# Gate/up biases of a mixture of experts: from matmuls on TensorE to additions on VectorE

## The chip, the cores and the metric

One NeuronCore of a Trainium2 chip runs the whole program, one residual block of an encoder (mixer and mixture of experts) for 512 tokens. The metric is device microseconds of one execution. Five engines work side by side: TensorE (PE; its weight loads are PEld), VectorE (DVE), ScalarE (ACT), GpSimd (POOL) and SyncE (SP), which only issues DMAs here. Semaphores tie them together.

## The reference

Only the experts matter here. Each of 512 tokens goes to 4 of 32 experts; `D_MODEL` and `D_EXPERT` are 1024, all in float32.

```python
    def expert_block(args):
        xb, e = args
        gu = xb @ w_gate_up[e] + b_gate_up[e]
        gate = jnp.minimum(gu[:, ::2], SWIGLU_LIMIT)
        up = jnp.clip(gu[:, 1::2], -SWIGLU_LIMIT, SWIGLU_LIMIT)
        act = (up + 1.0) * (gate * jax.nn.sigmoid(gate * SWIGLU_ALPHA))
        return act @ w_down[e] + b_down[e]
```

`b_gate_up` has 32 x 2048 elements. The change is to how the `+ b_gate_up[e]` is made.

## The kernel before

The first part of the program (the mixer: delta rule, attention, merge of both) ends near 800 us. Then come the router and the tables of which token goes to which expert, up to about 886 us, then the loop over 32 experts, then the tail with the sums over each token's four experts and the last norm.

**An expert.** Up to 96 tokens (`ROWS`), in three groups of 32 (`QUADS`). The gate/up weights come in eight chunks of 1 MB, the down weights in four. All twelve chunks have one place each in the buffer `ring`; SyncE issues the load of a chunk for expert n when a count (`gu_used`, `dn_used`) says that expert n - 1 has used it (`up_weights`, L486, and `down_weights`, L492). TensorE runs `expert(n)` (L1149): `up(n)` (L1106), 8 slices of 12 matmuls of 32 tokens x 512 columns each (each matmul shows as two records in the trace), then `down(n - 1)` (L1135), 96 matmuls of 32 x 256. The four matmuls of one group go to four column strips of the array, so each strip of 32 partitions of the PSUM tile `gu` holds another 512 of the 2048 gate/up columns, for the 32 tokens of the group.

**VectorE.** `activations(n)` (L2145) waits for all eight slices, reads `gu` twice with clamps (L2149 the even columns to `gb`, L2150 the odd ones to `ub`), multiplies, and takes ScalarE's sigmoid (`gate`, from `gb`). The second read releases `gu` for expert n + 1 (`gu_free`). `token_columns` transposes the next expert's gathered tokens in blocks of 32x32, `activation_columns` the activations, as soon as `down(n - 1)` has used the old ones.

**The biases.** In the merge, `bias_part` (L1941) splits the float32 biases three times into bfloat16 parts, which SyncE stores to `bias_dram`. In the expert loop `bias_rows` holds the parts of five experts (15 rows, in each of three groups of partitions); `bias_block` (L503) loads them, block b + 1 while block b is used, into two buffers by turns. After the first slice of `up`, twelve matmuls (L1130) with a 32x32 matrix `pick` of zeros and ones add the expert's three rows to every token's row. VectorE writes `pick` for the next expert (L2153) after its reads of `gu`. Because the buffer is chosen in Python, the loops on SyncE and TensorE are cut into seven.

**GpSimd** gathers the tokens of expert n + 2 from `h_rows` and scatters the outputs of expert n to `expert_rows`, with indirect DMAs.

**The tail.** While `up(31)` runs, SyncE issues the loads of `expert_rows` for the first two of the four slots (L561, 8 x 512 KB), then the four down chunks of expert 31 as `down(30)` uses the old ones, then the rows of the last two slots. VectorE adds the slots up one after the other (`add_slot`, `add_rows`), ScalarE and VectorE norm the result. What some experts have beyond 96 tokens would be done by further blocks (`extra`); here there are none.

The order of work on each engine is as written in the code.

## Time and profile before

| | |
|---|---|
| median of 3 runs | 1935.56 us (1934.43 to 1935.81) |
| span of the profiled execution | 1933.1 us |
| TensorE busy | 1894.0 us, 98% |
| VectorE busy | 587.9 us, 30% |
| ScalarE, GpSimd busy | 333.0 us, 264.1 us |
| DMA, whole span | 497.65 MB, mean 257 GB/s |
| mean granted TensorE clock | 0.990 |

The page gives no time of its own for the profiled execution beside its span. "Busy" counts the time in which an engine executes; for TensorE the ends of matmuls are modelled. The page's slices cut the span in 40 parts of 48.3 us: one digit is the busy share in tenths. A view of waits says who released whom; a landing time is from the issue of a DMA to its completion.

### The profile page before, as it was taken

The numbers are of one execution on the slowest core, as the hardware profiler recorded it, in microseconds if no ns is written. First come the engines' busy times: TensorE is split into PE (matmuls) and PEld (weight loads), VectorE is DVE, ScalarE is ACT, GpSimd is POOL, SyncE is SP. The second block draws the span as 40 slices with busy tenths as digits, with TensorE's granted clock in tenths as the row PEclk, the third lists the DMA queues.
The fourth block names the chain that finished last, engine by engine and source line by source line (L and its number), as shares of the span: only waits on it lengthen the run. The fifth ranks groups of instructions, "written<-read, shape, count | busy, mean of one in ns | idle before, by whom it ended". The sixth has DMA issues, their size and how long they took to land.

```text
span 1933.1 us, 41164 instructions
## 1 busy us (share of the span) xinstructions
PE 1894.0 (98%) x17590; PEld 870.7 (45%) x17590; DVE 587.9 (30%) x1077; ACT 333.0 (17%) x596; POOL 264.1 (14%) x306
## 2 busy tenths in 40 slices
PE   7999999999999999999999999999999999999996
PEld 4455555554555444454343434434343434343434
DVE  2463563635533110144121221212121212121226
ACT  3223323323233000021011010101011101011002
POOL 0010010000100000014122212121212121221200
PEclk9999999999999999997999999999999999999998
DMA  9211011111101322437999999999999999999995
GB/s 377 86 64 48 29 56 33 45 50 44 45 23 66 136 93 68 161 113 279 391 417 405 419 416 405 417 419 404 416 420 414 408 418 419 414 419 418 419 398 225
DMA packets 82948, 497.65 MB, mean 257 GB/s; under 512 B 15543, under 2 KB 16223, under 8 KB 28933
## 3 DMA queue, kind: packets, MB, share of 16 engines
q1 hardware_dynamic: 73364, 480.35, 62.1%
q0 software_dynamic: 9488, 15.94, 2.2%
q8 instruction: 70, 1.15, 0.2%
q14 instruction: 26, 0.21, 0.0%
HBM read 479.47 MB, written 24.92 MB: 261 GB/s over the span
## 4 chain that ended last, share of the span: by engine, by line
PE 93%; DVE 3%; DMA 1%; DVEq 1%; ACT 1%; issue 0%; SPq 0%; ACTq 0%
PE ps L1124 35%; PE ps L621 21%; PE ps L1144 17%; PE ps L616 10%; PE ps L641 2%; PE ps L840 2%; DVE arena L1577 1%; DVE arena L1580 1%; PE ps L1054 1%; DMA arena<-expert_rows 1%; PE ps L958 1%; PE ps L953 1%; PE ps L1130 1%; PE ps L933 0%; PE ps L725 0%
## 5 line engine op out<-in xcount | busy, mean ns | idle before, releaser
L1124 PE MATMUL ps<-arena 128*32 128x512 f32 x5952 | 652.4, 594 | 2.3 <-DVE pick L2153 2.3
L1124 PEld LDWEIGHTS ps<-arena 128*32 128x32 f32 x5952 | 190.7, 110 | 424.4 <-issue 419.3
L621 PE MATMUL ps<-hT,arena 128*128 128x512 f32 x768 | 350.8, 598 | 1.2 <-DVE arena L1580 0.9
L1144 PE MATMUL ps<-arena,hT 128*32 128x256 f32 x6144 | 340.3, 381 | 3.9 <-DMA arena<-in_w_dn 3.9
L1144 PEld LDWEIGHTS ps<-arena,hT 128*32 128x32 f32 x6144 | 201.0, 111 | 150.8 <-issue 25.7
L2149 DVE TENSOR_SCALAR arena<-ps 128x768 f32<-128x768 f32 x32 | 30.6, 958 | 627.4 <-PE ps L1124 627.4
L621 PEld LDWEIGHTS ps<-hT,arena 128*128 128x128 f32 x768 | 139.0, 191 | 144.3 <-issue 140.1
L2306 POOL DMA_INDIRECT expert_rows<-hT,six x90 | 90.4, 1005 | 695.5 <-ACT hT L1215 677.1
L1215 ACT ACTIVATE hT<-arena 128x768 f32<-128x768 f32 x31 | 48.4, 1560 | 443.4 <-DMA arena<-h_rows,gix 443.4
L621 PE MATMUL ps<-arena 128*128 128x512 f32 x256 | 118.5, 603 | 4.4 <-DVE arena L1577 2.2
L2294 POOL DMA_INDIRECT arena<-h_rows,gix x93 | 95.3, 1025 | 49.7 <-POOL gix L2291 27.2
L1215 ACT ACTIVATE arena<-ps 128x512 f32<-128x512 f32 (+4 forms) x114 | 61.4, 539 | 186.5 <-PE ps L840 99.3
L616 PE MATMUL ps<-arena 128*128 128x128 f32 (+3 forms) x352 | 84.5, 370 | 0.0
L1215 ACT ACTIVATE hT<-ps 128x768 f32<-128x768 f32 (+1 forms) x34 | 27.0, 793 | 291.4 <-PE ps L1144 283.2
L2166 DVE STREAM_TRANSPOSE hT<-arena 128x768 f32<-128x768 f32 x32 | 31.3, 978 | 145.7 <-PE ps L1144 145.6
L1577 DVE TENSOR_TENSOR arena<-arena,ps 128x128 f32<-128x128 f32 (+1 forms) x88 | 38.1, 433 | 107.4 <-PE ps L840 57.8
L621 PEld LDWEIGHTS ps<-arena 128*128 128x128 f32 x256 | 46.0, 190 | 53.3 <-issue 46.5
L1577 DVE TENSOR_TENSOR arena<-arena 128x768 f32<-128x768 f32 (+6 forms) x55 | 66.5, 1210 | 6.7 <-issue 4.6
L616 PEld LDWEIGHTS ps<-arena 128*128 128x128 f32 x352 | 52.8, 190 | 21.6 <-issue 17.3
L1580 DVE SCALAR_TENSOR_TENSOR arena<-arena,ps 128x512 f32<-128x512 f32 x24 | 15.6, 679 | 144.1 <-PE ps L616 143.7
L1519 ACT ACTIVATE arena<-arena 128x768 f32<-128x768 f32 x32 | 27.0, 843 | 187.6 <-DVE arena L2149 187.6
L1580 DVE SCALAR_TENSOR_TENSOR arena<-ps,cw,arena 128x511 f32<-128x511 f32 (+2 forms) x72 | 53.7, 745 | 9.2 <-ACT arena L1216 4.7
(254 smaller groups left out, 1289.7 us busy)
## 6 DMA issues: line engine op xcount, KB each, us to landing
arena<-in_w_gu SPq DMA_DIRECT2D x256, 1024.0 KB, 15.9
arena<-in_w_dn SPq DMA_DIRECT2D x128, 1024.0 KB, 15.4
arena<-in_w_pair SPq DMA_DIRECT2D x16, 1024.0 KB, 4.8
arena<-in_w_merge SPq DMA_DIRECT2D x16, 1024.0 KB, 5.0
expert_rows<-oaT SPq DMA_DIRECT2D x4, 2048.0 KB, 25.3
arena<-expert_rows SPq DMA_DIRECT2D x16, 512.0 KB, 13.7
arena<-in_x SPq DMA_DIRECT2D x8, 512.0 KB, 6.7
arena<-in_w_qb SPq DMA_DIRECT2D x4, 768.0 KB, 4.6
```

What stands on the lines that cost most here:

```text
L616: ins = pe.matmul(dst, lhsT, rhs, start=(k == 0), stop=(k == len(pairs) - 1))
L621: ins = pe.matmul(region(name)[:, cols], lhsT, rhs, start=(k == 0), stop=(k == n - 1))
L641: ins = pe.matmul(region(name)[0:m, :], w[:, k, j * P:j * P + m], hT[:, k, :], start=(k == 0), stop=(k == KD - 1))
L840: ins = pe.matmul(region(name)[p, c * CHUNK:(c + 1) * CHUNK], lhs[p, c, :], rhs[p, c, :], start=True, stop=True)
L1124: ins = pe.matmul(gu[32 * j:32 * (j + 1), g, :], columns[:, g, k, :], ring[k][:, 512 * j:512 * (j + 1)], start=(k == 0), stop=(k == KD - 1))
L1144: ins = pe.matmul(yd[32 * j:32 * (j + 1), g, 0:256], aT[:, g, 2 * c + k, :], ring[8 + c][:, D * k + 256 * j:D * k + 256 * (j + 1)], start= ...
L1215: return ac.activation(dst, src, ACT.Copy)
L1577: return dv.tensor_tensor(o, a, b, op)
L1580: return dv.scalar_tensor_tensor(out=o, in0=a, scalar=s, in1=b, op0=op0, op1=op1)
L2166: dv.transpose(aT.rearrange("p g b m -> p (g b m)"), act.rearrange("p g f -> p (g f)")).then_inc(aT_done, 1)
L2294: po.indirect_dma_start(out=xg[:, 256 * g:256 * (g + 1)], out_offset=None, in_=h2_dram.rearrange("r (j d) -> (r j) d", j=4), in_offset=bas ...
L2306: po.indirect_dma_start(out=y_dram.rearrange("r (j d) -> (r j) d", j=4), out_offset=bass.IndirectOffsetOnAxis(ap=six[:, g:g + 1], axis=0), ...
```

## The change

The bias is added by VectorE as it reads `gu`. The host now lays the biases out as columns: `bias_columns` (128 partitions x 32 experts x 16), loaded once. Partition 32 j + r holds, for each of 16 blocks of 32, the element that belongs to place r of strip j. `spread_bias(e)` copies the 16 columns of expert e and runs them through the 32x32 block transpose with a source that repeats each column 32 times (stride 0), so that every partition of strip j ends with the 512 biases of its strip: 256 for gate, 256 for up. `activations` then has two additions (PSUM plus `bias_rows`, repeated for the three groups), and the clamps behind them work in place in SBUF. Gone are the twelve bias products an expert, `pick`, the bfloat16 split, its stores, and all loads of `bias_block`. The loops on SyncE and TensorE are one piece again. The memset of `xg` on GpSimd waits for the end of the mixer instead of the split.

```diff
         def _(sp):
-            sp.dma_start(bfull, b_gu).then_inc(bias_ld, 16)
-            for n in range(4 * PAIRS + 8, 4 * PAIRS + 12):
+            sp.dma_start(bias_columns, b_gu).then_inc(bias_gu_in, 16)
+            for n in range(4 * PAIRS + 8, 4 * PAIRS + 18):
                 mixer_weights(n)
-            for part in range(3):
-                sp.wait_ge(bias_cast, part + 1)
-                sp.dma_start(bias_dram[:, part, :], bpart).then_inc(kept_st, 16)
-                mixer_weights(4 * PAIRS + 12 + 2 * part)
-                mixer_weights(4 * PAIRS + 13 + 2 * part)
...
-            bias_block(1)
-            for b in range(BIAS_BLOCKS):
-                begin = BIAS_EXPERTS * b
-                if b:
-                    up_weights(begin, begin, range(2))
-                    if b + 1 < BIAS_BLOCKS:
-                        bias_block(b + 1)
-                    up_weights(begin, begin, range(2, 8))
-                    down_weights(begin - 1, begin - 1)
-                with sp.Fori(begin + 1 if b else 2, min(begin + BIAS_EXPERTS, NE)) as e:
-                    up_weights(e, e, range(8))
-                    down_weights(e - 1, e - 1)
+            with sp.Fori(2, NE) as e:
+                up_weights(e, e, range(8))
+                down_weights(e - 1, e - 1)
...
         def _(pe):
                     ins.then_inc(gu_used, 1)
-                    if k == 0:
-                        for g in range(QUADS):
-                            for j in range(4):
-                                pe.matmul(gu[32 * j:32 * (j + 1), g, :], pick[32 * g:32 * (g + 1), :], bias_rows[block % 2][32 * g:32 * (g + 1), 512 * j:512 * (j + 1)],
-                                          start=False, stop=False)
...
         def _(dv):
+            def spread_bias(e):
+                dv.tensor_copy(bias_now, bias_columns[:, bass.ds(16 * e, 16)])
+                dv.drain()
+                dv.transpose(bias_rows, bias_now.unsqueeze(2).broadcast_to([P, 16, 32]))
+                dv.drain()
+
-            def activations(n, pick_next=True):
+            def activations(n):
                 dv.wait_ge(gu_used, 8 * n + 8)
-                g2 = gu.rearrange("p g (f two) -> p two (g f)", two=2)
-                dv.tensor_scalar(gb, g2[:, 0, :], LIMIT, None, ALU.min).then_inc(g_min, 1)
-                dv.tensor_scalar(ub, g2[:, 1, :], LIMIT, -LIMIT, ALU.min, ALU.max).then_inc(gu_free, 1)
-                if pick_next:
-                    at = PICK + n + 1 if not isinstance(n, int) or n < NE - 1 else PICK
-                    dv.tensor_copy(pick[:, :], sm[:, bass.ds(at, 1)].broadcast_to([P, 32])).then_inc(pick_done, 1)
+                g2 = gu.rearrange("p g (f two) -> p two g f", two=2)
+                for half, dst in enumerate((gb, ub)):
+                    ins = tt(dst.rearrange("p (g f) -> p g f", g=QUADS), g2[:, half],
+                             bias_rows[:, HALF_F * half:HALF_F * (half + 1)].unsqueeze(1).broadcast_to([P, QUADS, HALF_F]), ALU.add)
+                ins.then_inc(gu_free, 1)
+                dv.drain()
+                dv.tensor_scalar(gb, gb, LIMIT, None, ALU.min).then_inc(g_min, 1)
+                dv.tensor_scalar(ub, ub, LIMIT, -LIMIT, ALU.min, ALU.max)
                 dv.drain()
...
             with dv.Fori(1, NE - 1) as n:
                 activations(n)
                 token_columns(n + 1)
                 activation_columns(n)
+                spread_bias(n + 1)
...
         def _(po):
-            po.wait_ge(bias_cast, 3)
+            po.wait_ge(oa_done, 2 * PAIRS)
             po.memset(xg, 0.0).then_inc(xg_clear, 1)
-            po.memset(bcur, 0.0).then_inc(bias_clear, 1)
```

How the instructions stand on VectorE in the loop over experts 1 to 30. Names are of tiles: `ps` is PSUM (here `gu`), `arena` the SBUF buffer that holds nearly all others, `hT` the transposed or gathered operands. Before:

```order
L2149 TENSOR_SCALAR arena<-ps 128x768
L2150 TENSOR_SCALAR arena<-ps 128x768
L2153 ISA
L2153 COPY pick<-sm 128x32
L1580 SCALAR_TENSOR_TENSOR arena<-arena 128x768
L2157 REGISTER_ALU
L1577 TENSOR_TENSOR arena<-arena 128x3x32x8
L2143 STREAM_TRANSPOSE arena<-hT 128x768
L2165 REGISTER_ALU
L2166 STREAM_TRANSPOSE hT<-arena 128x768
```

and in the changed kernel:

```order
L1525 TENSOR_TENSOR arena<-ps,arena 128x768 x2
L2093 TENSOR_SCALAR arena<-arena 128x768
L2094 TENSOR_SCALAR arena<-arena 128x768
L1528 SCALAR_TENSOR_TENSOR arena<-arena 128x768
L2098 REGISTER_ALU
L1525 TENSOR_TENSOR arena<-arena 128x3x32x8
L2074 STREAM_TRANSPOSE arena<-hT 128x768
L2106 REGISTER_ALU
L2107 STREAM_TRANSPOSE hT<-arena 128x768
L2079 ISA
L2079 COPY arena<-arena 128x16
L2081 STREAM_TRANSPOSE arena<-arena 128x512
```

Two clamps from PSUM have become two additions from PSUM and two clamps in SBUF; the cast to `pick` is gone from the middle, and copy and transpose of the next expert's bias stand at the end, behind the transpose that waits for `down(n - 1)`.

On SyncE's queue, at the step from one block of five experts to the next, before:

```order
L544 COMPARE_AND_BRANCH
L490 DMA arena<-in_w_gu 128x2048 x2
L511 DMA csn<-bias_parts 16x2048 x3
L490 DMA arena<-in_w_gu 128x2048 x6
L496 DMA arena<-in_w_dn 128x2048 x4
```

The three bias loads stood between the second and the third chunk of the block's first expert. In the changed kernel the whole of it is one loop of eight `in_w_gu` and four `in_w_dn` loads an expert, and its last lines are followed by the tail:

```order
L508 REGISTER_ALU
L508 COMPARE_AND_BRANCH
L511 DMA hT<-in_norm_final 128x1024
L518 DMA arena<-in_token_row 128x512
L525 DMA arena<-expert_rows 128x1024 x8
L486 DMA arena<-in_w_dn 128x2048 x4
L525 DMA arena<-expert_rows 128x1024 x8
```

No load of the tail has moved against another.

## Rows read from the trace of the kernel before

**Rows 1.** the page's slices of the span, 40 equal ones: TensorE, DMA engines, rate

```profile
PE   7999999999999999999999999999999999999996
DMA  9211011111101322437999999999999999999995
GB/s 377 86 64 48 29 56 33 45 50 44 45 23 66 136 93 68 161 113 279 391 417 405 419 416 405 417 419 404 416 420 414 408 418 419 414 419 418 419 398 225
```

**Rows 2.** timeline of TensorE, one expert: start us, us, engine, line, operation

```profile
1074.89 18.23 PE L1124 MATMUL ps<-arena 128*32 128x512 f32 x168
1092.94 10.54 PE L1144 MATMUL ps<-arena,hT 128*32 128x256 f32 x192
1103.30 2.76 PE L1124 MATMUL ps<-arena 128*32 128x512 f32 x24
1105.99 0.42 PE L1130 MATMUL ps<-csn,pick 32*32 32x512 bf16 x12
1106.34 18.23 PE L1124 MATMUL ps<-arena 128*32 128x512 f32 x168
```

**Rows 3.** waits of TensorE, whole run: us in total, times, longest

```profile
PE ps L1144 <- DMA arena<-in_w_dn: 3.9, 1, 3.9
```

**Rows 4.** DMA issues in 945:977, 1400:1450, 1816:1850; last number: us to landing

```profile
arena<-in_w_gu SPq DMA_DIRECT2D x8, 1024.0 KB, 8.1
...
arena<-in_w_gu SPq DMA_DIRECT2D x12, 1024.0 KB, 16.0
...
arena<-in_w_gu SPq DMA_DIRECT2D x9, 1024.0 KB, 20.6
```

**Rows 5.** timeline of the tail, DMA queue and VectorE

```profile
1882.00 8.10 SPq L496 DMA_DIRECT2D arena<-in_w_dn  x4
...
1889.77 0.98 DVE L2166 STREAM_TRANSPOSE hT<-arena 128x768 f32<-128x768 f32 x1 [5.81 <-PE ps L1144]
...
1906.08 4.87 DVE L1580 SCALAR_TENSOR_TENSOR oaT<-arena,w,oaT 128x1024 f32<-128x1024 f32 x4 [2.63 <-DMA arena<-expert_rows]
```

**Rows 6.** timeline of the DMA queue, one block's bias load

```profile
1172.46 1.36 SPq L511 DMA_DIRECT2D csn<-bias_parts  x3
```

**Rows 7.** stretches of the loop: us, TensorE busy, its clock, DMA share, GB/s

```profile
1019.00:1025.00 6.00, 6.00 (x64) 1.00 1.04 324
1176.00:1184.00 8.00, 8.00 (x80) 1.00 1.02 337
1184.00:1198.00 14.00, 14.00 (x232) 1.00 1.01 420
1334.00:1344.00 10.00, 10.00 (x96) 1.00 1.02 338
1491.00:1505.00 14.00, 14.00 (x164) 1.00 1.02 367
1650.00:1661.00 11.00, 11.00 (x128) 1.00 1.01 402
```

**Rows 8.** the same view, stretches of the tail

```profile
1863.00:1878.00 15.00, 15.00 (x148) 1.00 0.99 389
1878.00:1894.00 16.00, 12.11 (x213) 0.96 0.96 360
```

**Rows 9.** groups by line and shape, VectorE, one expert, then the tail

```profile
L2149 DVE TENSOR_SCALAR arena<-ps 128x768 f32<-128x768 f32 x1 | 1.0, 958 | 20.1 <-PE ps L1124 20.1
...
L2143 DVE STREAM_TRANSPOSE arena<-hT 128x768 f32<-128x768 f32 x1 | 1.0, 979 | 0.1
...
L1577 DVE TENSOR_TENSOR oaT<-oaT,ps 128x768 f32<-128x768 f32 x4 | 3.8, 955 | 1.0 <-issue 1.0
```

**Rows 10.** timeline of TensorE, first slice of expert 1

```profile
912.89 4.48 PE L1124 MATMUL ps<-arena 128*32 128x512 f32 x24 [2.30 <-DVE pick L2153]
```

**Rows 11.** stretches around it, TensorE and its clock

```profile
913.00:917.00 4.00, 4.00 (x24) 0.57 0.93 286
917.00:921.00 4.00, 4.00 (x48) 1.00 0.62 214
```

More of the change, by code:

```diff
@@ L181, in build @@
         weight_dram = nc.dram_tensor("choice_weights", [SEQ * NE, 1], F32, kind="Internal").ap()
-        bias_dram = nc.dram_tensor("bias_parts", [NE, 3, 2 * DE], BF16, kind="Internal").ap()
         mk = sb("mk", [P, N_MASKS, P])
@@ L362, in build @@
         gate_done, merged = sem("gate_done"), sem("merged")
-        wo_in, row_in, bias_ld, bias_cast, kept_st = (sem(n) for n in ("wo_in", "row_in", "bias_ld", "bias_cast", "kept_st"))
+        wo_in, row_in, bias_gu_in, kept_st = (sem(n) for n in ("wo_in", "row_in", "bias_gu_in", "kept_st"))
         x2_done, h2_done, h2_st, x2T_done = (sem(n) for n in ("x2_done", "h2_done", "h2_st", "x2T_done"))
@@ L496, in down_weights @@
                     sp.dma_start(ring[c], w_dn_chunk(e, c)).then_inc(chunk_in[c], 16)
-            def up_bias(n, e):
-                sp.wait_ge(gu_used, 8 * n + (2 - 8))
-                for g in range(QUADS):
-                    sp.dma_start(bcur[32 * g:32 * g + 3, :], bias_dram[bass.ds(e, 1)].rearrange("o b f -> (o b) f")).then_inc(bias_gu_in, 16)
-            def bias_block(b):
-                rows = 32 if b == 1 else min(3 * BIAS_EXPERTS + 1, 3 * (NE - BIAS_EXPERTS * b))
-                if b == 1:
-                    sp.wait_ge(list_done, 1)
-                    sp.wait_ge(gu_used, 8)
-                if b > 1:
-                    sp.wait_ge(gu_used, 8 * (BIAS_EXPERTS * (b - 1) - 1) + 2)
-                for g in range(QUADS):
-                    sp.dma_start(bias_rows[b % 2][32 * g:32 * g + rows, :], bias_dram.rearrange("e b f -> (e b) f")[3 * BIAS_EXPERTS * b:3 * BIAS_EXPERTS * b + rows, :]).then_inc(bias_gu_in, 16)
             up_weights(0, 0, range(6))
-            sp.wait_ge(kept_st, 48)
-            sp.wait_ge(bias_clear, 1)
-            bias_block(0)
             def keep_rows(t):
@@ L1104, in weight_columns, with up @@
                 fill(ins, "wm")
-            def up(n, beside={}, picked=True, block=0):
+            def up(n, beside={}):
                 if not first(n):
@@ L1111, in up @@
                     pe.wait_ge(xT_done, n)
-                if first(n):
-                    pe.wait_ge(bias_gu_in, 16 * QUADS)
-                if picked:
-                    pe.wait_ge(pick_done, n + 1)
-                else:
-                    pe.wait_ge(bias_gu_in, 16 * QUADS * n - 16 * QUADS * (NE - BIAS_BLOCKS - 1))
                 for k in range(KD):
@@ L1126, in up @@
                     ins.then_inc(gu_used, 1)
-                    if k == 0:
-                        for g in range(QUADS):
-                            for j in range(4):
-                                pe.matmul(gu[32 * j:32 * (j + 1), g, :], pick[32 * g:32 * (g + 1), :], bias_rows[block % 2][32 * g:32 * (g + 1), 512 * j:512 * (j + 1)],
-                                          start=False, stop=False)
                     if k in beside:
@@ L1147, in down, with expert @@
                     ins.then_inc(dn_used, 1)
-            def expert(n, block=0):
-                up(n, block=block)
+            def expert(n):
+                up(n)
                 down(n - 1)
@@ L1159, in _ @@
             expert(1)
-            for b in range(BIAS_BLOCKS):
-                if b:
-                    pe.wait_ge(bias_gu_in, 16 * QUADS * (b + 1))
-                with pe.Fori(BIAS_EXPERTS * b if b else 2, min(BIAS_EXPERTS * (b + 1), NE)) as n:
-                    expert(n, b)
+            with pe.Fori(2, NE) as n:
+                expert(n)
             down(NE - 1)
@@ L2168, in _ @@
             token_columns(1)
-            dv.wait_ge(kept_st, 64)
+            dv.wait_ge(kept_st, 16)
+            dv.wait_ge(bias_gu_in, 16)
+            spread_bias(0)
             activations(0)
             activation_columns(0)
+            spread_bias(1)
             with dv.Fori(1, NE - 1) as n:
@@ L2213, in _ @@
                     with dv.If(j < extra):
+                        e = dv.value_load(lst[0:1, bass.ds(j + LIST, 1)], min_val=0, max_val=NE - 1)
+                        spread_bias(e)
                         token_columns(j + NE)
-                        activations(j + NE, pick_next=False)
+                        activations(j + NE)
                         activation_columns(j + NE)
@@ L2359, in constants @@
     small = np.zeros((P, SMALL + 4 * EXTRA), np.float32)
-    row = np.arange(P)[:, None] % 32
-    holds = np.where(row < 3 * BIAS_EXPERTS, row // 3, -1)
-    small[:, PICK:PICK + NE] = (holds == np.arange(NE)[None, :] % BIAS_EXPERTS) & (np.arange(P)[:, None] < 32 * QUADS)
     small[:, 128:128 + ROWS] = np.arange(ROWS).reshape(QUADS, 32)[:, ::-1].reshape(-1)
@@ L2405 @@
                       for j in range(KD)])
+    bias = np.asarray(b_gate_up)[0].reshape(NE, 4, 8, 32, 2).transpose(1, 3, 0, 4, 2).reshape(P, NE * 16)
     data = dict(
```

38 lines of the change are left out of this document (9 added, 29 removed).

## The prediction

> **What bounds the kernel now.** I read the page first: of 40 slices of the span, TensorE is at 9 tenths in nearly all, and from slice 20 on the DMA engines are too, at 400 to 420 GB/s [rows 1]. So the second half, the 32 experts, has two resources near full, and the question is which one the change relieves, and which one sets the end.
>
> The timeline of TensorE in one expert answers for TensorE [rows 2]. From 1074.89 to 1106.34, one expert takes 31.45 us, with no gap in the rows. Its parts: seven of eight slices of the gate/up products take 1092.94 - 1074.89 = 18.05 us (2.58 each), the down products 10.36, and the first slice with the twelve bias products behind it 1106.34 - 1103.30 = 3.04. The seven others cost 2.58, so the bias products cost 0.46 us on TensorE. In the whole loop TensorE waits for DMA once, in the last down products, 3.9 us [rows 3]. Up to there TensorE sets the pace.
>
> The DMA view answers for the loads. A weight load of 1 MB lands 8.1 us after its issue at 945 to 977 us, 16.0 at 1400 to 1450, and 20.6 at 1816 to 1850 [rows 4]. A load waits only for the ring slot to come free, so the landing time is the backlog of the DMA engines. It grows over the loop and nowhere drops back: from about 945 us the DMA engines always have work, and TensorE takes weights a little faster than they come. What TensorE lives on is the ring of twelve chunks: a chunk is asked for when the expert before has used it and is needed one period less one slice later, 31.45 - 2.58 = 28.9 us. Of that 8.3 us are left at the end. So the last down weights and the slot rows behind them, asked for from 1882 us on, stand in a queue that has not been empty for 900 us, and the final sums on VectorE start when slot rows land, at 1906.08 after a wait of 2.63 [rows 5]. The end of the kernel is therefore set by the **sum of the DMA work**, although TensorE is "98% busy".
>
> **What the change does, part by part.**
>
> *Bias products off TensorE.* 32 experts x 0.46 = 14.7 us of TensorE's path [rows 2]. They stood in the chain in every expert, so TensorE reaches its last down products 14.7 us sooner if nothing else stops it. The new period is 30.99 us.
>
> *Bias loads off the queue.* Six blocks of experts follow the first; five of their loads fall into the saturated time, three issues each, 16 rows x 4 KB an issue, that is 0.197 MB a block (the fifth 6 rows, 0.074 MB) [rows 6]. They cost far more than their bytes. Beside 420 GB/s in a quiet stretch, the stretches in which they land move 324, 337, 338, 367 and 402 GB/s over 6, 8, 10, 14 and 11 us [rows 7]. Lost bytes: 0.58, 0.66, 0.82, 0.74, 0.20 MB; with the bias's own bytes 0.77, 0.86, 1.02, 0.94, 0.27, and at 420 GB/s 1.8, 2.1, 2.4, 2.2, 0.7 us, together 9.2. The first and the last of these stretches also hold rows of gathers and scatters, which pass at a slightly lower rate, so I take 8.6. Bounds: by bytes alone 0.86 MB, 2.1 us; at most 9.2.
> The Trainium skill (SBUF — State Buffer, the DMA port swizzle) says that a load's rate depends on how many of 16 ports its partitions reach, four for partitions 0 to 15, about 109 GB/s, and that partitions 32 further on share them. By it the two loads on the same ports would take 0.131 MB / 109 GB/s = 1.2 us a block, 5.3 us in all, and the time would come out at 1927.7; the trace agrees in kind (a fifth of the rate gone for some ten us) and asks more.
>
> *Where these two meet.* Since the backlog never empties, a load less is worth its time at the end, and TensorE's 0.46 an expert is worth nothing there beyond the point where the backlog begins. What TensorE gains before it counts: two experts' bias products (0.92) and the step between the first two experts (below, 0.1 to 0.2), 1.1 us together. Then the tail: the last down weights are issued at 1882.00 because TensorE's progress releases them [rows 5], and in 1878 to 1894 the engines move only 360 GB/s, beside 389 just before [rows 8]; some of them had run dry. With TensorE 14.7 us ahead and the backlog deeper this hole closes: (389 - 360) x 16 / 389 = 1.2 us, and against the 420 GB/s of a quiet stretch 2.3; I take 1.5, nearer to the row beside it.
>
> *Does TensorE run dry?* Backlog growth from 8.1 to 20.6 is 12.5 us in some 28 experts, 8.6 of it the bias loads, leaving 0.14 an expert. At a period of 30.99 it becomes 0.14 + 0.46 = 0.60 an expert, 17 us in 28, so about 25 us at the end of the 28.4 that the ring allows. It is close, and only a stall earlier than the last two experts would cost anything new.
>
> *VectorE's new work.* Per expert: the two reads of PSUM become additions with a second operand. A tensor_tensor of 128x768 with one operand in PSUM takes 955 ns in the tail, beside 958 for the clamp that reads PSUM now [rows 9]; no change. The two clamps move to SBUF: between half and all of 958 ns each. A copy of 16 columns stands in for a cast of 32 columns, nothing; the transpose of 128x512 is below the 979 ns of one of 128x768 [rows 9]. Sum: at most 2 x 0.96 + 0.98 = 2.9 us more, on an engine that waits 20.1 us of the period for the products. The cover: products of expert n are read while the down products of n - 1 run, 10.36 us, and gate/up banks are freed after the two additions, 1.9 us, as now. The spreading stands behind the transpose of the activations and before a wait of 20 us. In the last expert VectorE waits 5.81 us with its product done [rows 5]; the clamps' 1.9 fit. Only between experts 0 and 1 nothing covers: TensorE waited 2.30 us for the two reads and the cast there [rows 10]; without the cast 0.1 to 0.2 less.
>
> *Before the experts.* The three splits of the biases on VectorE and their stores stand beside the merge's matmuls, and of TensorE's waits only one is for a DMA [rows 3]. Nothing is gained, and the single load of columns is as large as the one it replaces.
>
> **Sum:** 8.6 + 1.1 + 1.5 = 11.2 us. The profiled execution has a span of 1933.1, 2.5 below the median of 1935.56; the page gives no other time for it, so I take these 2.5 as lying around the span. Predicted: span 1921.9, time 1924.4.
>
> **Rivals.**
> 1. *TensorE's path sets the end after all* (the tail follows the last down products, not the slot rows). For it: TensorE's gap-free timeline. Against it: VectorE waited for rows, not for TensorE. Gain 14.7 + 0.2, time 1920.7.
> 2. *Bias loads cost little more than their bytes* (the dips are something else that stays, such as the fetch of code at a loop's end). 2.1 + 1.1 + 1.5 = 4.7, time 1930.9. Against it: the dips come at each of the five blocks, and the smallest block has the smallest.
> 3. *Nothing to measure*: the deeper backlog makes the slot rows of the tail land late by as much as the loads gave back, and the bias terms are at their lower bound: 2.1 + 1.1 and no hole closed, less what the rows lose; time 1932 to 1936. Against it: the queue serves in order, and its sum is smaller.
> 4. *Slower*: the ring's 28.4 us are used up long before the end; TensorE waits in each expert, and behind a wait its clock is low. Behind the wait of 2.30 us the first slice took 4.48 us [rows 10], beside 2.58: the granted clock is 0.57 in 913 to 917 us, so mostly the 1.2 GHz level, and 1.00 from 917 on [rows 11]. That is 1.9 us an expert lost on TensorE's own path, which ends at 1920.7 without it; eight such experts make it a loss, twelve give 1920.7 + 12 x 1.9 = 1943.5. Against it: the ring would have to be used up by expert 20, from 8.1 to 28.4 us, 1.0 an expert instead of 0.60, and each slow slice lets the loads catch up.
>
> **Chances.** DMA work sets the end, as forecast: 0.60 (own range 1921.5 to 1928). Rival 1: 0.18. Rival 2: 0.14. Rival 3: 0.04. Rival 4: 0.04. What can be told from no change is about 0.2%, 3.9 us. Range for 8 in 10: from rival 1's 1920.7, less the 0.7 us by which two of the runs may differ, 1920.0, to 1930.0, which leaves out the last us of rival 2, and rivals 3 and 4. Faster by over 0.2%: 0.60 + 0.18 + 0.13 of rival 2 = 0.91; same: 0.01 + 0.04 = 0.05; slower 0.04.
>
> **What would show it.** Right: a period of 31.0 us between slices of successive experts; landing times that climb evenly, without steps, to 22 to 27 us; no dips below 390 GB/s in the loop; TensorE waiting more than 3.9 us for the last down weights; VectorE's last slot sum starting about 11 us sooner. Wrong: a TensorE wait inside the loop before expert 29 (rival 4), a climb below 20 us (rival 1), dips that remain (rival 2), or a period above 31.2, which would say that the bias products had been cheaper than 0.46.

## The result and the profile after

| | before | after |
|---|---|---|
| median | 1935.68 us (1934.43 to 1935.81) | 1923.64 us (1921.35 to 1925.91) |
| ratio | | 0.9936, 95% interval 0.9924 to 0.9948 |
| span of the profiled execution | 1933.1 us | 1923.9 us (that execution took 1925.91) |
| TensorE busy | 1894.0 us | 1877.7 us |
| VectorE busy | 587.9 us | 634.5 us |
| DMA | 497.65 MB | 495.45 MB |

12.0 us less, 0.6%. Forecast were 1924.4 us and a range of 1920 to 1930.

The page's slices of the span after (TensorE, DMA engines, rate), beside [rows 1]:

```profile
PE   7999999999999999999999999999999999999995
DMA  9211111111101412337999999999999999999995
GB/s 374 89 66 31 43 45 50 45 51 44 45 10 39 177 66 88 116 131 275 370 420 418 420 417 419 418 420 419 417 420 418 420 418 420 418 419 419 418 400 210
```

By the busy digits nothing has changed: both are at 9, as before. The third row has. In the loop it read 404, 405, 408 where the bias loads passed; now it stays at 417 to 420.

TensorE's timeline of one expert, beside [rows 2]:

```profile
1070.48 20.81 PE L1081 MATMUL ps<-arena 128*32 128x512 f32 x192
1091.08 10.57 PE L1096 MATMUL ps<-arena,hT 128*32 128x256 f32 x192
1101.44 8.79 PE L1081 MATMUL ps<-arena 128*32 128x512 f32 x80
```

One expert now takes 1101.44 - 1070.48 = 30.96 us instead of 31.45. The down products take 10.36 as before, the eight slices 20.60 instead of 21.09.

TensorE's waits, beside [rows 3] and [rows 10]:

```profile
PE ps L1096 <- DMA arena<-in_w_dn: 8.9, 1, 8.9
...
PE ps L1081 <- DVE arena L1525: 2.3, 1, 2.3
```

In the expert loop there is still one wait for weights, for the last down products, and it has grown from 3.9 to 8.9 us: TensorE reached its end earlier, the weights not as much. (A new one of 0.6 us stands ahead of the experts, for `in_w_cq`.) Between experts 0 and 1 TensorE waits for the additions as it had waited for the cast.

DMA issues in 945:977, 1400:1450 and 1780:1830, the last number being the time to landing, beside [rows 4]:

```profile
arena<-in_w_gu SPq DMA_DIRECT2D x8, 1024.0 KB, 9.1
...
arena<-in_w_gu SPq DMA_DIRECT2D x11, 1024.0 KB, 16.5
...
arena<-in_w_gu SPq DMA_DIRECT2D x14, 1024.0 KB, 24.3
```

The backlog of the DMA engines ends higher than before (20.6), though less is loaded: TensorE uses weights faster.

The tail, SyncE's queue, VectorE and TensorE, beside [rows 5]:

```profile
1867.93 8.10 SPq L486 DMA_DIRECT2D arena<-in_w_dn  x4
...
1876.13 8.20 SPq L525 DMA_DIRECT2D arena<-expert_rows  x8
...
1884.53 12.07 PE L1096 MATMUL ps<-arena,hT 128*32 128x256 f32 x192 [8.88 <-DMA arena<-in_w_dn]
...
1896.85 4.87 DVE L1528 SCALAR_TENSOR_TENSOR oaT<-arena,w,oaT 128x1024 f32<-128x1024 f32 x4 [7.46 <-DMA arena<-expert_rows]
```

The last down weights are asked for 14.1 us sooner (1882.00 before), but the sum of the third slot starts only 9.2 us sooner (1906.08 before), behind a wait of 7.46 us instead of 2.63. Everything behind it is as long as before. So 14 us gained on TensorE have become 9 here (12 by the medians), and the rest is waiting for DMA.

Rates at the place of one former bias load, then in three stretches before VectorE's wait for slot rows ends at 1896.85: the 50 us that end 10 us before it, those 10 us, and the whole last 50 (us, TensorE busy, its loads, VectorE, ScalarE, GpSimd, clock, DMA share, GB/s), beside [rows 7, 8], first after:

```profile
1176.00:1184.00 8.00, 8.00 (x81) 2.86 (x74) 0.00 (x0) 1.57 (x1) 0.00 (x0) 1.00 1.02 419
...
1837.00:1887.00 50.00, 41.12 (x552) 21.65 (x548) 21.94 (x27) 3.21 (x4) 3.02 (x3) 0.94 0.99 399
1887.00:1897.00 10.00, 10.00 (x180) 6.13 (x176) 2.54 (x3) 0.34 (x1) 0.00 (x0) 0.97 0.74 297
1847.00:1897.00 50.00, 41.12 (x564) 21.43 (x560) 18.93 (x22) 2.00 (x3) 2.53 (x3) 0.93 0.93 374
```

then before, at the same distances from that addition:

```profile
1846.00:1896.00 50.00, 46.11 (x632) 20.48 (x628) 16.85 (x22) 3.31 (x4) 3.01 (x3) 0.97 0.99 391
1896.00:1906.00 10.00, 10.00 (x156) 5.81 (x152) 7.34 (x7) 0.00 (x0) 0.00 (x0) 0.82 1.01 400
1856.00:1906.00 50.00, 46.11 (x616) 20.75 (x612) 18.80 (x21) 2.46 (x3) 3.01 (x3) 0.93 0.99 388
```

The dip of 337 GB/s is gone. The tail's hole has not closed, it has moved. Up to 10 us before the addition (399 - 391) x 50 / 417 = 1.0 us are gained, and in the last 10 us (400 - 297) x 10 / 417 = 2.5 us are lost: the DMA engines were busy for 0.74 of that time, before for all of it. Over the whole 50 us after stands (388 - 374) x 50 / 417 = 1.7 us worse. So the last part of the 7.46 us of waiting is not behind a full queue. The share is a mean over 16 engines; that some were idle already while others still moved parts of the third slot's rows would fit it, but the trace does not name the engines.

VectorE's forms after (line, shapes, count | busy, mean ns | idle before), beside [rows 9]:

```profile
L1525 DVE TENSOR_TENSOR arena<-ps,arena 128x768 f32<-128x768 f32 x64 | 58.3, 953 | 584.2 <-PE ps L1081 584.2
...
L2081 DVE STREAM_TRANSPOSE arena<-arena 128x512 f32<-128x512 f32 x32 | 22.8, 711 | 2.4
...
L2093 DVE TENSOR_SCALAR arena<-arena 128x768 f32<-128x768 f32 x32 | 17.9, 560 | 3.0
L2094 DVE TENSOR_SCALAR arena<-arena 128x768 f32<-128x768 f32 x32 | 17.8, 555 | 0.0
```

An addition from PSUM costs 953 ns, what the clamp from PSUM had cost (958); a clamp in SBUF 0.56 us. VectorE's new work is 2 x 0.56 + 0.71 + 0.13 = 1.96 us an expert.

### The profile page after: what moved, and what is told of

Same layout as the page of the kernel before. It is cut to its first block, busy times and chain, and to the rows that moved or that the text cites. A ratio compares the mean times of both kernels' runs of the same rounds, so it can differ in the third digit from the quotient of the medians.

```text
span 1923.9 us, 40758 instructions
## 1 busy us (share of the span) xinstructions
PE 1877.7 (98%) x17206; PEld 948.9 (49%) x17206; DVE 634.5 (33%) x1168; ACT 333.3 (17%) x596; POOL 262.0 (14%) x305
## 2 busy tenths in 40 slices
DMA packets 82217, 495.45 MB, mean 258 GB/s; under 512 B 15188, under 2 KB 15868, under 8 KB 28256
## 4 chain that ended last, share of the span: by engine, by line
PE 92%; DVE 3%; DMA 1%; DVEq 1%; SPq 1%; ACT 1%; issue 1%; ACTq 0%
PE ps L1081 34%; PE ps L584 21%; PE ps L1096 17%; PE ps L579 10%; PE ps L604 2%; PE ps L803 2%; DMA arena<-expert_rows 1%; DVE arena L1525 1%; DVE arena L1528 1%; PE ps L1017 1%; PE ps L921 1%; PE ps L916 1%; PE ps L896 0%; PE ps L688 0%; PE ps L773 0%
## 5 line engine op out<-in xcount | busy, mean ns | idle before, releaser
L1081 PEld LDWEIGHTS ps<-arena 128*32 128x32 f32 x5952 | 233.4, 110 | 396.5 <-issue 393.0
L1096 PEld LDWEIGHTS ps<-arena,hT 128*32 128x32 f32 x6144 | 240.2, 110 | 115.2 <-issue 27.6
L1525 DVE TENSOR_TENSOR arena<-ps,arena 128x768 f32<-128x768 f32 x64 | 58.3, 953 | 584.2 <-PE ps L1081 584.2
L1525 DVE TENSOR_TENSOR arena<-arena 128x768 f32<-128x768 f32 (+5 forms) x53 | 62.0, 1172 | 6.2 <-issue 0.2
```

Source lines behind the costliest of these rows:

```text
L1081: ins = pe.matmul(gu[32 * j:32 * (j + 1), g, :], columns[:, g, k, :], ring[k][:, 512 * j:512 * (j + 1)], start=(k == 0), stop=(k == KD - 1))
L1096: ins = pe.matmul(yd[32 * j:32 * (j + 1), g, 0:256], aT[:, g, 2 * c + k, :], ring[8 + c][:, D * k + 256 * j:D * k + 256 * (j + 1)], start= ...
L1525: return dv.tensor_tensor(o, a, b, op)
```

## The experiments

**Theory:** two paths end close together. One is the sum of the DMA work, the other TensorE's products with VectorE's sums behind them. The later one sets the end, so undoing one half of the change should lift one path only. **Rivals:** TensorE's time counts in full (and the loads for their bytes), or the bias loads count for everything. Medians of before, which ran beside each group of experiments, were 1935.36, 1935.64, 1935.92 and 1936.27 us. Every experiment is an edit of the kernel after. "Over after" is against its 1923.64.

| kernel | edit | us | ratio to before, 95% | over after |
|---|---|---|---|---|
| after_again | none | 1923.60 | 0.9937, 0.9923 to 0.9950 | 0.0 |
| e0_both | products and loads back | 1933.98 | 0.9988, 0.9980 to 0.9997 | 10.3 |
| e1_loads | bias loads back | 1934.15 | 0.9989, 0.9980 to 0.9997 | 10.5 |
| e2_products | products back, 32 experts | 1933.45 | 0.9984, 0.9975 to 0.9993 | 9.8 |
| e2_half | products back, experts 2 to 15 | 1923.88 | 0.9944, 0.9932 to 0.9957 | 0.2 |
| e3_vector | spreading four times | 1924.17 | 0.9935, 0.9920 to 0.9950 | 0.5 |
| e1_wide | loads: 1 x 128 partitions x 1.5 KB | 1926.62 | 0.9959, 0.9946 to 0.9973 | 3.0 |
| e1_full3 | loads: 3 x 128 x 512 B | 1926.58 | 0.9957, 0.9943 to 0.9970 | 2.9 |
| e1_three | loads: 3 x 64 x 1 KB | 1933.00 | 0.9987, 0.9978 to 0.9996 | 9.4 |
| e1_strided | loads: 3 x 16 x 4 KB, 8 apart | 1931.19 | 0.9975, 0.9966 to 0.9984 | 7.5 |
| e4_tail | third slot by tiles | 1920.27 | 0.9923, 0.9909 to 0.9937 | -3.4 |
| e4_order | e4_tail, down weights first | 1926.45 | 0.9950, 0.9936 to 0.9963 | 2.8 |

A figure "over after" is good to about 2 us, and to about 3 where only five executions stand behind it (e1_wide, e1_full3, e4_tail, e4_order). By the ratios, which compare each kernel with its own before, e2_half comes to 1.5 over after, e1_wide and e1_full3 to 4.5 and 4.1, and the three other forms of the loads (e1_strided, e1_three, e1_loads) to 7.5, 9.9 and 10.3.

### The loads alone

```diff
+            def spent_block(b):
...
+                for g in range(QUADS):
+                    sp.dma_start(spare[32 * g:32 * g + rows, :], x[3 * 16 * b:3 * 16 * b + rows, :]).then_inc(spent_in, 16)
...
-            with sp.Fori(2, NE) as e:
-                up_weights(e, e, range(8))
-                down_weights(e - 1, e - 1)
+            for b in range(7):
+                begin = 5 * b
+                if b:
+                    up_weights(begin, begin, range(2))
+                    if b + 1 < 7:
+                        spent_block(b + 1)
...
```

> The changed kernel with the bias loads of blocks 1 to 6 put back (same issues, same rows of 4 KB, same places in the queue, to a buffer that nobody reads; the rows are rows of x). TensorE has no bias products. Theory (the sum of the DMA work sets the end): the loads cost at the end what they cost the queue, 8.6 us or a little more, so 1923.6 + 8.6 = 1932.2; the landing time climbs in steps again and reaches the ring's 28.4 us near expert 24, and TensorE waits inside the loop. Rival 1 (TensorE's path sets the end): the loads are hidden, 1923 to 1925. Rival 2 (bias loads cost their bytes only): 2.1 us, 1925.7.

1934.15 us. TensorE's waits for weights, then the landing of gate/up weights in 1400:1450 and 1780:1830, then the sum of the third slot, in e1_loads:

```profile
PE ps L1117 <- DMA arena<-in_w_dn: 11.1, 1, 11.1
...
PE ps L1102 <- DMA arena<-in_w_gu: 1.6, 7, 0.3
```

```profile
arena<-in_w_gu SPq DMA_DIRECT2D x12, 1024.0 KB, 21.8
...
arena<-in_w_gu SPq DMA_DIRECT2D x12, 1024.0 KB, 27.9
```

```profile
1903.00 4.87 DVE L1549 SCALAR_TENSOR_TENSOR oaT<-arena,w,oaT 128x1024 f32<-128x1024 f32 x4 [9.68 <-DMA arena<-expert_rows]
```

Landing climbs until the ring is used up (27.9 of 28.4 us); then TensorE waits, 1.6 us in seven small pieces. The loads alone bring the end back to within 1.2 us of before, with TensorE still fast. TensorE's gain is worth almost nothing while they are there.

### The products alone, in all experts and in fourteen

```diff
                     ins.then_inc(gu_used, 1)
+                    if k == 0 and products:
+                        for g in range(QUADS):
+                            for j in range(4):
+                                pe.matmul(gu[32 * j:32 * (j + 1), g, :], pick[32 * g:32 * (g + 1), :], spent[32 * g:32 * (g + 1), :], start=False, stop=False)
...
```

Both operands are zeros.

> The changed kernel with twelve bf16 products of zeros behind the first slice of every expert, as before the change; no bias loads. Theory: TensorE reaches the last down products 15 us later, its 8.9 us of waiting there are used up and the rest shows, with the 1.1 us of the first experts: 1923.6 + 15.5 - 8.9 + 1 = about 1931; the landing time at the end of the loop is about 12 us instead of 24.9. Rival 1 (TensorE's path sets the end in full): 1923.6 + 15.5 = 1939. Rival (products are free because the queue is the bound alone): 1924.

> The same twelve products of zeros, but in experts 2 to 15 alone: 14 x 0.49 = 6.9 us on TensorE. Theory: 6.9 is less than the 8.9 us that TensorE waits for the last down weights, so the end stays within 1 us, 1923.6 to 1924.6, and that wait falls from 8.9 to about 2 us. Rival 1 (TensorE's path): 1930.5.

With the products in every expert, 1933.45 us, where about 1931 was expected. The theory had counted the 8.9 us that TensorE waits in after as slack, but the distance between the two ends was 15.7 - 9.8 = 5.9 us. That is nearer to VectorE's wait of 7.46, less the 1.4 us that VectorE waits longer here for TensorE's late products in the tail (1.68 instead of 0.25). Landing in 1400:1450 and 1780:1830, and the tail:

```profile
arena<-in_w_gu SPq DMA_DIRECT2D x12, 1024.0 KB, 8.6
...
arena<-in_w_gu SPq DMA_DIRECT2D x11, 1024.0 KB, 9.8
```

```profile
1891.51 10.57 PE L1101 MATMUL ps<-arena,hT 128*32 128x256 f32 x192 [1.15 <-ACT hT L1168]
1894.24 4.87 DVE L1533 SCALAR_TENSOR_TENSOR oaT<-arena,w 128x1024 f32<-128x1024 f32 x4
1899.24 9.87 DVE L1533 SCALAR_TENSOR_TENSOR oaT<-arena,w,oaT 128x1024 f32<-128x1024 f32 x8
```

The backlog hardly grows (8.9 us at 945:977, 9.8 at the end, where about 12 was expected), no engine waits for DMA in the tail, and the three early sums stand back to back. Here the other path is seen undisturbed: down products of expert 30, the transpose behind them, sums. It ends at 1933.45, and without 32 x 0.49 = 15.7 us of products it would, as an estimate, end at 1917.8. The growth of 12.5 us in the landing before [rows 4] came nearly all from the bias loads: with the same period and no loads it is 0.9.

With the products in experts 2 to 15 only, 14 x 0.49 = 6.9 us of TensorE time cost 0.2 us by the medians (1.5 by the ratios), far from the 6.9 of rival 1. TensorE's wait for the last down weights fell from 8.9 to 1.3 us, close to the 2 expected. Landing in the same two windows, and the third slot:

```profile
arena<-in_w_gu SPq DMA_DIRECT2D x11, 1024.0 KB, 9.3
...
arena<-in_w_gu SPq DMA_DIRECT2D x12, 1024.0 KB, 16.7
```

```profile
1894.66 4.87 DVE L1535 SCALAR_TENSOR_TENSOR oaT<-arena,w,oaT 128x1024 f32<-128x1024 f32 x4 [0.24 <-DMA arena<-expert_rows]
```

The wait for slot rows has shrunk from 7.46 to 0.24 us: both paths end together here. The third slot's rows landed no later than in after, although TensorE had released their loads later.

### Both back

The edit is those of e1_loads and e2_products together.

> Both put back: the bias loads of blocks 1 to 6 and the twelve products of zeros in every expert. Theory: the kernel before in all that costs time, so its time within 1 us, 1935 to 1936.5; the two alone give 8.6 and 7.5 of 12, so they must not add up (8.6 + 7.5 = 16). Rival (something else of the change made part of the gain: the uncut loops, the split in the merge): below 1933.

1933.98 us, landing 18.7 us in 1780:1830. Alone the two cost 10.5 and 9.8, together 10.3. That is the later of two ends, not a sum. The theory had wanted 1935 to 1936.5, the rival below 1933, and the result lies between them. What is still missing to before (1935.36 beside it) is 1.4 us by the medians and 2.3 by the ratio, whose interval, 0.9980 to 0.9997, leaves out 1. So a small part of the gain comes from something that no run put back (the bias split in the merge and its stores are candidates); which, stays open.

### VectorE's work

```diff
-                dv.transpose(bias_rows, bias_now.unsqueeze(2).broadcast_to([P, 16, 32]))
-                dv.drain()
+                for _ in range(4):
+                    dv.transpose(bias_rows, bias_now.unsqueeze(2).broadcast_to([P, 16, 32]))
+                    dv.drain()
```

> The kernel after with the block transpose that spreads the bias made four times instead of once in every expert, 3 x 0.71 = 2.1 us more VectorE work in each of 32 experts (67 us in the whole), at the place where the prediction said that it is hidden (before a wait of 18.78 us for the products). Theory, nothing changes: 1923 to 1924.5, the wait shrinks to 16.7 us, the period stays 30.96. Rival, VectorE's additional work of the change does lie on the path somewhere in each expert: 30 x 2.1 = 63 us slower for all of it, or some 6 us for a tenth of it. Between experts 0 and 1, where nothing covers VectorE, the spreading stands ahead of expert 0's products and should not show either.

1924.17 us. VectorE's timeline of one expert in e3_vector:

```profile
1215.79 1.82 DVE L1525 TENSOR_TENSOR arena<-ps,arena 128x768 f32<-128x768 f32 x2 [16.41 <-PE ps L1081]
...
1227.26 3.07 DVE L2082 STREAM_TRANSPOSE arena<-arena 128x512 f32<-128x512 f32 x4
```

67 us more work changed nothing that can be told; the wait for the products took it (18.78 us in after, 16.41 here).

### Why a load of 0.2 MB costs 2 us

The forecast had priced these loads by the dips, without a reason for them. Five runs (e1_loads and four more) with the same bytes at the same places of the queue ask for it. The first block, near 911 us, has twice the rows in each form: in e1_loads its loads go to 32 partitions, in e1_strided to 32 that lie 4 apart.

```diff
e1_wide
+                sp.dma_start(spare[:, 0:24 * rows], x.rearrange("a (b c) -> (a b) c", c=1024)[P * (b % 4):P * (b % 4) + P, 0:24 * rows]).then_inc(spent_in, 16)
e1_strided
+                    sp.dma_start(spare[at:at + step * (rows - 1) + 1:step, :], x[3 * 16 * b:3 * 16 * b + rows, :]).then_inc(spent_in, 16)
e1_three
+                    sp.dma_start(spare[64 * (g % 2):64 * (g % 2) + 64, 512 * (g // 2):512 * (g // 2) + 16 * rows], x[64 * ((b + g) % 8):64 * ((b + g) % 8) + 64, 0:16 * rows]).then_inc(spent_in, 16)
e1_full3
+                    sp.dma_start(spare[:, 256 * g:256 * g + 8 * rows], x[P * ((b + g) % 4):P * ((b + g) % 4) + P, 0:8 * rows]).then_inc(spent_in, 16)
```

> The kernel after (1923.64) with the same bytes that the bias loads moved (0.197 MB for a block, 0.393 for the first), at the same places of SyncE's queue and in a loop cut into the same seven pieces, but as one load over all 128 partitions instead of three over 16 partitions each. e1_loads, with three loads over 16 partitions each, took 1934.15, 10.5 more than after. Theory: what cost time was that few partitions were written. Then only the bytes are left, 0.86 MB at 420 GB/s, 2.1 us, and a fetch of rows that is none worse than a weight's: 1925.7 to 1926.5, no stretch of the loop far below 400 GB/s. Rival A, it is the cut loops and waits on SyncE's queue or the number of loads: as e1_loads, 1933 to 1935 for the cuts, and between the two if it goes by the number of loads (three against one): 1927 to 1929. The output is the reference's; the loaded rows are used by nothing.

> As e1_loads (three loads a block, 16 rows of 4 KB each), but each load's 16 rows go to 16 partitions 8 apart (start 0, 4 and 1) instead of 16 in a row, so bytes, number of loads, rows and row size are the same and only the places in SBUF differ. Theory A, neighbouring partitions are what is slow (the Trainium skill, SBUF — State Buffer, the DMA port swizzle, says that partitions 0 to 15 reach only four of 16 ports): the cost falls well below the 10.5 us of e1_loads, to about half or less, 1926 to 1929. Theory B, what is slow is 16 rows of 4 KB in one load, however they are placed, because such a load occupies the DMA engines unevenly: the cost stays, 1933 to 1935. The output is the reference's; the loaded rows are used by nothing.

> As e1_loads (three loads at each of the six places, 0.197 MB together, the same cut loops), but each load goes to 64 partitions with 1 KB each instead of 16 partitions with 4 KB each. So far: one load over 128 partitions costs 3.0 us against after (e1_wide, 1926.62), three over 16 partitions 8 apart cost 7.5 (e1_strided, 1931.19), three over 16 neighbouring partitions 10.5 (e1_loads, 1934.15). Theory, a load is dear when it writes few partitions with long rows: three loads over 64 partitions cost little more than the one over 128, 1926.5 to 1928. Rival, the number of loads makes the larger part of the 7.5 that e1_strided still costs: 1929.5 to 1931.5. The output is the reference's; the loaded rows are used by nothing.

> Three loads at each of the six places, as in e1_loads and e1_three, with the same bytes together, but each goes to all 128 partitions with 512 bytes each. e1_three (three loads over 64 partitions) took 1933.00, so its theory of few partitions with long rows fell, and e1_wide (one load over 128) took 1926.62. They differ in the number of loads and in whether a load covers all 128 partitions. Theory A, a load over a part of the partitions is what slows the weights beside it (a weight load covers all 128, and in the trace of e1_three the stretch in which its loads pass moves 290 to 383 GB/s with the engines busy all the time): three loads over all partitions cost little more than one, 1926 to 1928, and no stretch falls below 390 GB/s. Theory B, the number of loads does it: 1931 to 1934, with dips as in e1_three. The output is the reference's; the loaded rows are used by nothing.

One load over all 128 partitions cost 3.0 us, so the cut loops were not it. Spreading the 16 rows helped by 3 of 10.5 us, less than half: neither theory of e1_strided held. Then 64 partitions cost 9.4, not to be told from 10.5, and the theory of few partitions with long rows fell with it. Three loads over all partitions cost 2.9, no more than one. What remains is one distinction: **a load over all 128 partitions cost about its bytes, the same bytes over some of them 2.5 to 3.5 times as much by the medians** (1.7 to 2.5 times by the ratios). The two wide kernels' intervals reach down to 0.9946 and 0.9943, that of after up to 0.9948, so their 3 us are not sharp; after_again, at 1923.60, says that after itself had not moved. At 417 GB/s all the bytes take 3.0 us with the block loaded near 911 us (0.39 + 0.86 = 1.25 MB) and 2.1 us without it, as the forecast had them; the runs cannot tell these apart. The stretch in which the loads of one block pass, 1175:1187 us (us, TensorE busy, its loads, VectorE, ScalarE, GpSimd, clock, DMA share, GB/s), in e1_loads, e1_strided, e1_three, e1_full3 and e1_wide:

```profile
1175.00:1187.00 12.00, 12.00 (x148) 5.67 (x144) 3.23 (x5) 2.43 (x2) 0.00 (x0) 1.00 1.02 354
```

```profile
1175.00:1187.00 12.00, 12.00 (x160) 6.12 (x156) 4.14 (x6) 2.41 (x2) 0.00 (x0) 1.00 1.01 377
```

```profile
1175.00:1187.00 12.00, 12.00 (x128) 4.89 (x124) 1.00 (x2) 1.58 (x1) 0.74 (x2) 1.00 1.02 362
```

```profile
1175.00:1187.00 12.00, 12.00 (x176) 6.76 (x172) 5.78 (x7) 2.42 (x2) 0.00 (x0) 1.00 1.02 419
```

```profile
1175.00:1187.00 12.00, 12.00 (x181) 6.91 (x177) 6.35 (x7) 2.29 (x2) 0.00 (x0) 1.00 1.01 421
```

The DMA share is the same in all five: the engines are busy all the time, only each byte takes longer. That holds for the weights beside the bias too: by the trace's records of single packets, a weight packet of 8 KB in this stretch took 371 ns on average in e1_loads, 349 in e1_strided and 366 in e1_three, beside 315 in e1_full3, 314 in e1_wide and 317 in after.
The Trainium skill (SBUF — State Buffer, the DMA port swizzle and the section on issuing two DMAs) says that partitions 0 to 63 reach only 8 of 16 ports and that only one transfer spanning all 128 reaches all 16. The order of e1_three and e1_full3 agrees in kind. Its figures do not cover the size of e1_three: at half the rate the bytes would take twice their 3.0 us, so it would cost an estimated 6.0 us, and it cost 9.4. For e1_loads, with 4 ports for 16 partitions and 8 for the first block's 32, the same reckoning gives an estimated 3.0 x (2 x 0.39 + 4 x 0.86) / 1.25 = 10.1 us, and it cost 10.5. By the ports of e1_full3, all 16, nothing is lost, and nothing that can be told was.

### The tail

```diff
-                    sp.dma_start(yin[k][:, t, :], slot_rows(k, t)).then_inc(slot_in[k] if k < TOPK - 1 else rows_in[t], 16)
+                    sp.dma_start(yin[k][:, t, :], slot_rows(k, t)).then_inc(slot_in[k] if k < TOPK - 2 else tile_in[t] if k < TOPK - 1 else rows_in[t], 16)
...
+                    for t in range(NT):
+                        dv.wait_ge(tile_in[t], 16)
+                        add_rows(k, t)
...
```

> The kernel after, with slot 2 of the tail waited for tile by tile (one semaphore for each of its four loads) instead of once for all four. In the profile after, the sum of slot 2 starts at 1896.85 behind a wait of 7.46 us for its rows, takes 4.87 us and the last slot and the norm follow. Theory, the rows of slot 2 land one after another about 1.2 us apart (0.5 MB at 420 GB/s), so three of four additions move beside the landing: up to 3.6 us sooner, 1920 to 1921.5. Rival, the rows of the last slot, queued right behind, land so late that its tiles set the end: the four additions move ahead and wait there, 1922.5 to 1923.6.

1920.27 us, as the theory had it. The third slot in e4_tail:

```profile
1891.54 4.98 DVE L1529 SCALAR_TENSOR_TENSOR oaT<-arena,w,oaT 128x1024 f32<-128x1024 f32 x4 [2.96 <-DMA arena<-expert_rows]
```

It now starts when the first of four tiles is there, waits 2.96 us for it instead of 7.46, and ends at 1896.52, in after at 1901.72. This is the fastest kernel of the study: 0.9923 of before.

```diff
-            for k in range(2):
-                early_slot(k)
             down_weights(NE - 1, NE - 1)
-            for k in range(2, TOPK):
+            for k in range(TOPK):
                 early_slot(k)
```

> e4_tail, and in SyncE's queue the four down chunks of expert 31 stand ahead of the eight loads of the first two slots instead of behind them. In the profile after, TensorE waits 8.9 us for these chunks, because 4 MB of slot rows stand before them in a queue with 25 us of backlog. Theory, the sum of the DMA work is the same, but TensorE's last down products (12 us with the wait) start up to 8 us sooner, and nothing but slot rows is outstanding at the end; as the rows of the last slot hang on the last scatter, which follows the last down products, the end comes 3 to 6 us sooner than in e4_tail: 1915 to 1918. Rival, the DMA queue's sum sets the end in either order, and the loads of the first slots, now behind a wait for the down products of expert 30, leave the queue less full: as e4_tail or up to 3 us slower.

1926.45 us, 6.2 slower than e4_tail, beyond even the rival's 3. TensorE's last down products and the sums of the first three slots, then two stretches of the tail, in e4_order:

```profile
1878.28 10.57 PE L1095 MATMUL ps<-arena,hT 128*32 128x256 f32 x192 [1.14 <-ACT hT L1162]
1888.41 4.88 DVE L1527 SCALAR_TENSOR_TENSOR oaT<-arena,w 128x1024 f32<-128x1024 f32 x4 [7.51 <-DMA arena<-expert_rows]
1894.22 9.87 DVE L1527 SCALAR_TENSOR_TENSOR oaT<-arena,w,oaT 128x1024 f32<-128x1024 f32 x8 [0.93 <-DMA arena<-expert_rows]
```

```profile
1855.00:1865.00 10.00, 10.00 (x100) 3.75 (x96) 0.00 (x0) 0.00 (x0) 0.00 (x0) 1.00 0.71 294
1865.00:1880.00 15.00, 13.86 (x244) 9.18 (x239) 8.15 (x12) 1.65 (x2) 0.00 (x0) 1.00 0.74 285
```

The same stretches in e4_tail:

```profile
1855.00:1865.00 10.00, 10.00 (x107) 3.86 (x100) 0.46 (x1) 0.00 (x0) 0.00 (x0) 1.00 0.96 380
1865.00:1880.00 15.00, 9.84 (x184) 6.85 (x176) 9.86 (x15) 1.66 (x2) 0.00 (x0) 0.98 0.99 392
```

The theory fell in an instructive way. TensorE's last products lost their wait of 8.1 us and it brought nothing. The slot loads, now behind a wait for `down(30)`, had been what kept the engines busy meanwhile: ((380 - 294) x 10 + (392 - 285) x 15) / 417 = 5.9 us of transfers were not made in these 25 us. That this nearly equals the 6.2 us is not the whole account. By the landing times in the traces the third slot's rows were complete at 1899.3, in e4_tail at 1895.2, 4.1 us later, and VectorE did not wait for them: its third sum follows the second without a gap and ends at 1904.09, 7.6 us later than in e4_tail. What ends last here is VectorE's own chain, three sums of 5 us each, of which the first could start only at 1888.41 (1878.71 in e4_tail), because the first slot's rows were asked for late. So this run shows what it costs to hold back loads, partly in the queue and partly in the sums that hang on them; it does not show by itself that the sum of the DMA work sets the end. For that stand e2_half and e1_loads.

## Why the prediction was right, by its steps

- **What bounds the kernel.** Right: the DMA work, though TensorE is 98% busy (e2_half, e1_loads). Only in the last 10 us are the engines no longer all busy (share 0.74), so there the sum of the transfers is not the whole account. One thing was not seen: before, the other path ended at about 1933.5 (e2_products), only some 2 us ahead, so both halves of the change were needed. The forecast's own row had it, as VectorE's wait of 2.63 us for slot rows [rows 5]. That the forecast gave TensorE's 14.7 us no value was right only because they were removed too.
- **Bias products off TensorE**, 0.46 us an expert: measured 0.49, period 30.96 for 30.99.
- **Bias loads**, 8.6 us: put back alone they cost 10.5 us by the medians, above the upper bound of 9.2, but with 2 us of noise on the figure the 8.6 is not refuted. The dips were the right place to look. They leave out the block loaded near 911 us, 0.39 MB, 0.9 us by bytes alone. Whether it cost anything is open: just behind it the engines had time to spare, with a share of 0.62 in 917:921 [rows 11].
- **Onset**, 1.1 us: not seen by itself. Between experts 0 and 1 TensorE waited 2.30 us before and 2.3 after, so the 0.1 to 0.2 us of that step did not come.
- **Hole in the tail**, 1.5 us: this step failed. The rates over the last 50 us are 1.7 us worse than before, not better, because the engines were no longer all busy at the end (share 0.74 in the last 10 us, 1.01 before). The wait for the last down products grew to 8.9, as said.
- **The sum.** Forecast 11.2, found 12.0. Only the loads' 10.5 was measured by itself. e0_both, in which the early TensorE is taken back too and with it onset and hole, costs no more than the loads alone (10.3), so neither small term was seen in a time, and 1.4 to 2.3 us of the gain belong to nothing in the sum. That the forecast came so near is in part luck: a loads term that came out larger stands against two small terms that did not show.
- **Does TensorE run dry?** No: landing 24.3 us at 1780 to 1830, forecast about 25 at the end, of 28.4. Of the forecast's two parts one was wrong: growth was shared out as 8.6 by loads and 0.14 an expert besides. e2_products shows 0.9 in some 27 experts, 0.03 an expert.
- **VectorE**, at most 2.9 us more, hidden: 1.96, and three times as much spreading changed nothing.
- **Rival 1** (TensorE's path sets the end): its mechanism exists and, by the estimate above, ends at 1917.8, not 1920.7, being the earlier path. **Rival 2** (bytes alone): e1_loads against e1_wide, 10.5 against 3.0. **Rival 3**: the slot rows gave back some 1.7 us of rate in the tail, not the gain. **Rival 4** (ring used up, slow clock behind the waits): with landing at 27.9 us in e1_loads the ring was used up, and TensorE lost 1.6 us in seven waits of at most 0.3, at a clock of 1.00 (below). A wait that long and a slow slice in every expert, on which the 1943.5 rested, did not show in any run.
- **What would show it.** Period 30.96 (31.0 forecast), landing up to 24.3 (22 to 27), the wait for the last down weights 8.9 (over 3.9) all came. The third slot's sum started 9.2 us sooner in one profile of after and 1906.08 - 1893.15 = 12.9 in the other (after_again), around the forecast's 11; the two executions differ by 3.7 us in themselves.

## What to carry to other kernels

When two engines are near full, look at the time from issue to landing of loads that wait only for their buffer: if it grows and never falls, the end hangs on the transfers, and time taken off the busier-looking engine is worth nothing beyond the distance to the second path. So find out both ends before pricing an edit; the gain of two edits that relieve one path each is not the sum of theirs (10.5 and 9.8 alone, 10.3 together). In a full queue make even small loads over all 128 partitions, and put no wait in front of loads that could fill it, least of all of those on which a chain of sums hangs. Where an engine waits for the last transfers, look at the DMA share of that stretch: below 1 it says that the queue was no longer full.

## What the runs showed of the hardware that was not expected

- In a queue at 420 GB/s, 1.25 MB of small loads in six blocks (the first with twice the rows) cost 9.4 us over 64 partitions each, 10.5 over 16, 7.5 over 16 that lie 8 apart, and 2.9 to 3.0 over 128, in one load or three. The engines count as busy all the while, with 354 to 377 GB/s instead of 420, and the weights' own packets of 8 KB take 349 to 371 ns instead of 314 to 317. Why a narrow load slows the wide ones beside it, no view here shows; it stays open.
- A wait for DMA can end at engines that are not all busy: in the last 10 us before the third slot's rows were there their share was 0.74 in after (297 GB/s) and 1.01 in before (400 GB/s).
- Waits of at most 0.3 us for weights left the clock at 1.00 (2.4 GHz), while the slice behind the one wait of 2.30 us had run at 0.57, mostly the 1.2 GHz level [rows 10, 11]. The stretch of e1_loads in which five of the seven lie (us, TensorE busy, its loads, VectorE, ScalarE, GpSimd, clock, DMA share, GB/s):

```profile
1700.00:1860.00 160.00, 158.65 (x1944) 61.54 (x1937) 40.30 (x50) 16.00 (x15) 29.97 (x37) 1.00 1.01 419
```

- An addition of two operands, one in PSUM, costs VectorE 953 ns, what a clamp of one operand from PSUM costs (958); from SBUF the clamp of 128x768 takes 0.56 us.
